# Gate slot first in the first products of the dense stages, zero matmuls behind the sums of six norms, and one pair of loads in the other order

## The reference

```python
def modulated_norm(x, g, shift, scale):
    return rmsnorm(x, g) * (1 + scale) + shift
def swiglu(h, wg, wu, wd):
    return (jax.nn.silu(h @ wg) * (h @ wu)) @ wd
...
    for l in range(DEPTH):                       # DEPTH = 2
        h = modulated_norm(x, norm_g[l, 0], sh1, sc1)
        x = x + 0.5 * g1 * swiglu(h, ffn_wg[l, 0], ffn_wu[l, 0], ffn_wd[l, 0])
        h = modulated_norm(x, norm_g[l, 1], sh2, sc2)
        m = attn_pool_mixer(h, ...) if l % 2 == 0 else short_conv_mixer(h, ...)
        x = x + g2 * m
        h = modulated_norm(x, norm_g[l, 2], sh3, sc3)
        x = x + 0.5 * g3 * swiglu(h, ffn_wg[l, 1], ffn_wu[l, 1], ffn_wd[l, 1])
```

## Time and profile before

| | us |
|---|---|
| median of 3 runs | 1722.42 |
| lowest, highest | 1721.34, 1727.29 |
| the profiled execution, its own time | 1724.32 |
| its span in the profile | 1722.5 |
| PE busy in the span | 1609.0 (93%) |
| mean granted clock of PE | 0.955 |

### The profile page before, as it was taken

How to read it: one execution, slowest core, us unless ns; L and a number is a source line. 1 busy time by engine, 2 the same in 40 slices (tenths; PEclk the granted TensorE clock), 3 DMA queues, 4 the chain that set the end, 5 groups by cost and what they waited for, 6 DMA issues and landing times.

```text
span 1722.5 us, 29138 instructions
## 1 busy us (share of the span) xinstructions
PE 1609.0 (93%) x12267; PEld 1522.4 (88%) x12267; DVE 1130.3 (66%) x1156; ACT 780.7 (45%) x808; POOL 17.2 (1%) x24
## 2 busy tenths in 40 slices
PE   5999989789999999998988999899899889999995
PEld 3999988579999999998988999898788689999994
DVE  2777777567777677756645454664664568888983
ACT  2433344434333443334434333444454447777772
POOL 0000000300000000000000000000000000000000
PEclk8999999889999999999998999999999889999997
DMA  9897766336878587863625555354332518898980
GB/s 323 273 329 278 271 242 242 125 123 248 289 270 313 173 292 270 313 196 126 196 98 171 177 188 177 126 171 117 110 123 98 218 54 347 342 357 346 357 327 26
DMA packets 202482, 379.90 MB, mean 221 GB/s; under 512 B 12185, under 2 KB 157470, under 8 KB 190110
## 3 DMA queue, kind: packets, MB, share of 16 engines
q1 hardware_dynamic: 202398, 378.70, 62.4%
HBM read 377.63 MB, written 1.05 MB: 220 GB/s over the span
## 4 chain that ended last, share of the span: by engine, by line
PE 84%; DVE 7%; ACT 4%; DMA 3%; issue 1%; SPq 0%; ACTq 0%; DVEq 0%
PE ps L579 20%; PE ps L580 19%; PE ps L581 19%; PE ps L1183 3%; PE ps L1185 3%; PE ps L1184 3%; DVE wlo L1678 3%; ACT whi L1300 2%; PE ps L1208 2%; PE ps L1209 2%; PE ps L1210 2%; DMA ada_raw<-in_w_ada_dram 2%; PE ps L690 2%; DVE rstd L1744 1%; PE ps L705 1%
## 5 line engine op out<-in xcount | busy, mean ns | idle before, releaser
L1678 DVE TENSOR_TENSOR wlo<-raw,whi 128x2048 fp32r<-128x2048 f32 (+1 forms) x191 | 432.9, 2267 | 346.5 <-ACT whi L1300 346.4
L579 PE MATMUL ps<-hhi,whi 128*128 128x256 f32 (+1 forms) x2024 | 587.7, 290 | 27.8 <-DVE hlo L1688 16.7
L580 PE MATMUL ps<-hlo,whi 128*128 128x256 f32 (+1 forms) x2024 | 579.1, 286 | 0.0
L581 PE MATMUL ps<-hhi,wlo 128*128 128x256 f32 (+1 forms) x2024 | 578.7, 286 | 0.0
L1300 ACT ACTIVATE whi<-raw 128x2048 fp32r<-128x2048 f32 (+1 forms) x191 | 360.1, 1886 | 209.9 <-PE ps L581 164.2
L579 PEld LDWEIGHTS ps<-hhi,whi 128*128 128x128 f32 (+1 forms) x2024 | 395.1, 195 | 35.8 <-issue 26.5
L580 PEld LDWEIGHTS ps<-hlo,whi 128*128 128x128 f32 (+1 forms) x2024 | 395.1, 195 | 1.8 <-issue 1.4
L581 PEld LDWEIGHTS ps<-hhi,wlo 128*128 128x128 f32 (+1 forms) x2024 | 394.8, 195 | 0.0
L579 PE MATMUL ps<-hidhi,whi 128*128 128x256 f32 x704 | 201.0, 286 | 2.8 <-DVE wlo L1805 2.8
L581 PE MATMUL ps<-hidhi,wlo 128*128 128x256 f32 x704 | 199.2, 283 | 0.0
L580 PE MATMUL ps<-hidlo,whi 128*128 128x256 f32 x704 | 199.2, 283 | 0.0
(11 more groups left out here) (276 smaller groups left out, 2449.7 us busy)
## 6 DMA issues: line engine op xcount, KB each, us to landing
ada_raw<-in_w_ada_dram SPq DMA_DIRECT2D x72, 1024.0 KB, 5.3
raw<-in_ffn_wg_dram SPq DMA_DIRECT2D x44, 1024.0 KB, 5.6
raw<-in_ffn_wu_dram SPq DMA_DIRECT2D x44, 1024.0 KB, 5.4
raw<-in_ffn_wd_dram SPq DMA_DIRECT2D x44, 1024.0 KB, 6.8
raw<-in_w_in_dram SPq DMA_DIRECT2D x18, 1024.0 KB, 5.4
raw<-in_w_exp_gate_dram SPq DMA_DIRECT2D x16, 1024.0 KB, 6.6
raw<-in_w_exp_up_dram SPq DMA_DIRECT2D x16, 1024.0 KB, 8.6
raw<-in_w_exp_down_dram SPq DMA_DIRECT2D x16, 1024.0 KB, 4.8
```

The costliest lines, as they stand in the source:

```text
L579: pe.matmul(o, wh, xh, start=start, stop=False, skip_group_check=shared)
L580: pe.matmul(o, wh, xl, start=False, stop=False, skip_group_check=shared)
L581: return pe.matmul(o, wl, xh, start=False, stop=stop, skip_group_check=shared)
L1678: dve.tensor_tensor(wlo[s][:, 0:width], raw[s][:, 0:width], whi[s][:, 0:width].bitcast(F32), ALU.subtract).then_inc(split[s], 1)
```

## The change

Four edits. (1) In `first_two` the loop over k does both halves of slot 0, with `used[0]` behind it; then comes the wait for slot 1 and both halves of slot 1. The callers wait for slot 1 there and no longer ahead of the loop. (2) `norm_sums` takes a number of matmuls on the tile of zeros (256 columns each, into the free half of bank 6) and runs them behind the sums: 30 ahead of mix0, mix1 and blk2, 18 ahead of ffn1, ffn2 and ffn3, none at the start, ahead of the router and at the end. (3) Before them PE waits for `mod_ready` (the vectors of the modulation that have been turned through bank 6). (4) For ffn3 alone SP issues the first up load (slot 1) ahead of the first gate load (slot 0).

```diff
                 def pair(c):
-                    load(0, c + b[0], wg(c))
-                    load(1, c + b[1], wu(c))
+                    for s in ((1, 0) if stage == "ffn3" and isinstance(c, int) and c == 0 else (0, 1)):
+                        load(s, c + b[s], (wg, wu)[s](c))
...
-            def first_two():
+            def first_two(second):
...
                 for k in range(KT):
                     wait("h_ready")
-                    for s in range(2):
-                        product(s, k, 0)
-                for s in range(2):
+                    for m in range(2):
+                        mm = product(0, k, m, k == 0 and m == 0)
+                mm.then_inc(used[0], 1)
+                second()
+                for m in range(2):
                     for k in range(KT):
-                        mm = product(s, k, 1)
-                    mm.then_inc(used[s], 1)
+                        mm = product(1, k, m, k == 0)
+                mm.then_inc(used[1], 1)

             def first_units(freed_by):
-                for s in range(2):
-                    slot_ready(s)
-                    own(s)
-                first_two()
+                slot_ready(0)
+                own(0)
+                first_two(second=lambda: (slot_ready(1), own(1)))
...
-            def norm_sums():
+            def keep_clock(n, vectors):
+
+                if n:
+                    own(6)
+                    pe.wait_ge(sem("mod_ready"), vectors)
+                for _ in range(n):
+                    pe.matmul(ps[:, 6, T:2 * T], zeros[:, :], zeros[:, :].rearrange("p (o n) -> p o n", o=1).to_broadcast([P, 2, P]),
+                              start=True, stop=True)
+
+            def norm_sums(fill=0, vectors=0):
...
                 mm.then_inc(sem("stat_ready"), 1)
                 frees(7, "stat_read")
+                keep_clock(fill, vectors)
...
-                pe.wait_ge(split[1], b0[1] + 1)
-                if ch:
-                    pe.wait_ge(sem("hid_done"), ch)
-                first_two()
+
+                def second():
+                    pe.wait_ge(split[1], b0[1] + 1)
+                    if ch:
+                        pe.wait_ge(sem("hid_done"), ch)
+
+                first_two(second)
...
-            norm_sums()
+            norm_sums(30, 7)
             first_units(("sq_done", "sq_done"))
...
-            norm_sums()
+            norm_sums(18, 9)
             chunked("ffn1", 9)
-            norm_sums()
+            norm_sums(18, 14)
             chunked("ffn2", 14, 4)
-            norm_sums()
+            norm_sums(30, 18)
...
-            norm_sums()
+            norm_sums(18, 18)
             chunked("ffn3")
-            norm_sums()
+            norm_sums(30, 18)
```

More of the change, by code:

```diff
@@ L601, in feature_major, with product @@
                 mm.then_inc(used[s], 1)
-            def first_two():
-                def product(s, k, m):
+            def first_two(second):
+                def product(s, k, m, start):
                     c = slice(k * 2 * P + m * P, k * 2 * P + (m + 1) * P)
                     return three(ps[:, s, m * T:(m + 1) * T], whi[s][:, c], wlo[s][:, c], hhi[:, k, :], hlo[:, k, :],
-                                 k == 0, k == KT - 1)
+                                 start, k == KT - 1, shared=True)
                 for k in range(KT):
                     wait("h_ready")
-                    for s in range(2):
-                        product(s, k, 0)
-                for s in range(2):
+                    for m in range(2):
[3 more added lines that the diff above has]
+                for m in range(2):
                     for k in range(KT):
-                        mm = product(s, k, 1)
-                    mm.then_inc(used[s], 1)
+                        mm = product(1, k, m, k == 0)
+                mm.then_inc(used[1], 1)
             def first_units(freed_by):
-                for s in range(2):
-                    slot_ready(s)
-                    own(s)
-                first_two()
+                slot_ready(0)
+                own(0)
+                first_two(second=lambda: (slot_ready(1), own(1)))
                 for s in range(2):
```

## The result

| | before | after |
|---|---|---|
| median of 4 runs each, one chip | 1721.88 us | 1704.55 us |
| lowest, highest | 1721.3, 1727.29 | 1700.56, 1705.66 |
| the profiled execution, its span | 1724.32, 1722.5 | 1700.56, 1698.8 |

The ratio of after to before is 0.9892 with a 95% interval of 0.9874 to 0.9911. By the medians the kernel after is 17.3 us faster, where 15.6 were worked out; the interval allows 15.3 to 21.7. The profiled execution is the fastest of the four, 4 us under their median. Of all runs in this document one, of double fill, fell into a slower state of the chip (1784.29 us at a mean clock of 0.833) and is left out of the comparisons. In the kernel after, L1678, L1688, L690, L1323, L1772 and L1300 are L1692, L1702, L700, L1337, L1786 and L1314; L690 is now the fill.

A forecast was written before the change was run, and what follows sets the result against it. PE was taken as the bound, so gains lie where it idles or runs at the lower clock. 7.5 + 6.2 + 1.9 = 15.6 us off the median of 1722.42 gave 1707 us; range 1701 to 1715.

The forecast's parts named there:

- Part 1, what the fill costs: Ahead of six stages' first products: each new zero matmul takes PE 0.12 us, 30 take 3.6, 18 take 2.2, all hidden.
- The rival of a slow fill: Each zero matmul waits for the one before, at 0.38 us; the kernel gets slower, 1737 us; chance 0.03.
- Part 1, what it gives: First products of mix0, ffn1, ffn2, mix1 and blk2: the clock holds, 12.0 us each, 11.6 in blk2; together 7.5 us.
- The rival that the clock falls all the same: In most stages the zeros don't keep the clock up and 7.5 us are lost: 1714.5 us; chance 0.12.
- I take nothing: ffn3's first products: 2.5 us of idle remain behind the zeros, so no clock gain counted; 1.6 us more if it held.
- Part 2, slot 0 first: gate(1) in four dense stages: slot 0 is released earlier, the old wait of 1.75 us goes; 6.2 us gained, ends 5.0 and 7.0.
- the chain of up(1): In ffn2, from silu times up through the hidden parts to the end of slot 1's wlo: 5.47 us.
- The new wait: At up(1), next late once gate(1) no longer waits: 0 to 0.2 us in each of four dense stages.
- Part 3, the swap: Norm ahead of ffn3: with up loaded first, PE's sums run without a stop and end 1.9 us earlier; ends 0 and 1.9.
- more isn't there, since PE ends unit 15 at 897.97: Norm ahead of ffn3: the gain from loading up first can't exceed 1.9 us, as PE's sums can't start sooner.

The follow-up runs named there:

- double fill: The changed kernel with 60 and 36 matmuls on zeros in place of 30 and 18: 1715.04 us over nine runs, ratio 0.9967.
- fill alone: The kernel before plus the matmuls on zeros in six stages and the wait for `mod_ready`, old order of products and loads: 1712.18 us, ratio 0.9954.
- without the swap: The changed kernel with the loads of ffn3 in the old order, gate ahead of up: 1708.95 us, ratio 0.9935.
- after, once more: The changed kernel, nothing altered, measured again on the chip of the kernel with zeros at two more places: 1702.65 us, ratio 0.9894.
- half fill: The changed kernel with 15 and 9 matmuls on zeros in place of 30 and 18: 1708.64 us, ratio 0.9934.
- more fill: The changed kernel with 34 zero matmuls for 18 in ffn3, 40 more in mix0's and 20 in mix1's output products: 1701.53 us, ratio 0.989.
- order alone: The kernel before with only slot 0 first in the first products, no new zeros, old loads: 1714.47 us, ratio 0.997.

## Why the prediction was right, point by point

**The forecast** was 15.6 us less, 1707 in all; measured were 17.3 and 1704.55, inside the range of 1701 to 1715. The mechanism held in both main parts.

**Part 1, what the fill costs.** Right. 0.12 each was taken and 0.12 measured for one more (0.13 on the mean of 18), and PE had 0.2 to 0.5 us left in the five stages that I named. The rival of a slow fill is out. Double fill confirms the price from the other side: 10.5 us for what its sum made 11.4.

**Part 1, what it gives.** Right in five stages: 12.0 us each and 11.6 in blk2 were forecast, 11.97 to 12.00 and 11.64 stand in the windows, and the five gained 7.7 us where 7.5 were written. The rival that the clock falls all the same is out for these: behind at most 0.51 us of idle it held 37 times in 37. One reading under this part was wrong. From the clock of 1.00 in the microsecond from 381, ahead of ffn1, I took that matmuls on zeros count as work. But in that profile the clock stays up through the whole idle piece behind the zeros and goes down only 1.4 us after the first product (383.95). Windows of before:

```profile
383.00:384.00 1.00, 0.05 (x1) 1.00 1.05 422
385.00:386.00 1.00, 1.00 (x8) 0.70 0.07 16
```

So the row shows nothing of the zeros. That they keep the clock is shown by the kernels with and without them.

**ffn3: the step that failed.** "I take nothing" rested on likeness: 2.5 us of idle remain, as much as ffn1 and ffn2 had when they fell. The estimate of the idle piece was right (2.43). The inference that such a piece loses the clock was too sure. Of four profiles with 18 zeros and 2.42 or 2.43 us there, the clock held in three (after, fill alone, without the swap) and fell in one (after, once more). Against the 13.62 us of before the term is 1.66 in the three and 0.48 in the one, about 1.4 on the mean. It is the largest part of what the sum lacked.

**Part 2, slot 0 first.** Right, and the chain step by step: gate(1) had 0.87 us in hand for 0.9 forecast; the chain of up(1) took 602.56 - 597.08 = 5.48 us for 5.47. The new wait is 0.05, in the lower half of the 0 to 0.2 that I gave, so that four stages give 6.8 and not 6.2. By the medians it alone gave 6.0, with an interval that holds both.

**Part 3, the swap.** Right for the profile shown: 1.92 us for 1.9. But "more isn't there, since PE ends unit 15 at 897.97" was bound to that execution. Where mix1 ends earlier, PE comes sooner and the load doesn't, and the swap is worth 3.0 to 3.2. Alone it gave 2.9 by the medians. I had read a distance from one profile as if it were a property of the kernel. The down load, moved up, didn't hold anything up: it landed by 882.46, 8.6 us behind its issue, and ACT stood 5.08 us for it, yet the sums ran without a stop. With gate and down in flight, gate took 5.3 us from issue to landing and down 8.6; with up between them before, gate took 5.4, up 8.0 and down 9.4, and the up load that now goes alone took 5.2. So loads in flight together slow each other, and gate and down landed no later with two than with three. That agrees with the Trainium skill, "DMA: Bandwidth & Descriptors", section "Issuing engines are not separate DMA queues", as cited in the prediction.

**Not foreseen.** In ffn2 some 0.57 us are lost again behind the first products (from up(1) to the next norm's sums 178.8 us for 178.1). They go at the starts of three later gate products (632.66, 668.48 and 704.20), 0.14 to 0.23 at each. Five profiles have 178.8 or 178.9 there and seven 178.1 to 178.3, among these half, double and more fill, which have all edits; the cause stays open. And I took the six norms for the only places with a changing clock, while in these two profiles 6.4 us of the difference come from other places. Against one profile of each kernel 23.7 us would have been read, not 17.3.

## What to carry to other kernels

Idle time of the bound engine that can't be cut can still be filled: matmuls on zeros into a free bank hold the clock for the real work behind. They cost nothing while they fit, and 0.12 us each from the first one that doesn't. Fill until what remains idle is a few tenths of a us: with 2.4 us left, the same steps held the clock in one execution and lost it in another. For a wait that is moved, work out the chain that is late next (here right to 0.05 us), and take a distance between two engines from more than one execution before you call it the kernel's.

## What was not expected of the hardware

The fall of the clock behind one and the same steps isn't fixed. In the twelve profiles, with six norms each, sorted by the idle piece of PE in front of the first product:

| idle ahead of the first product | clock held | clock fell |
|---|---|---|
| 0 to 0.51 us | 37 | 0 |
| 1.29 us | 2 | 0 |
| 2.09 to 2.43 us | 4 | 11 |
| 2.69 to 3.0 us | 1 | 3 |
| 3.5 to 4.6 us | 0 | 14 |

Where the clock fell, the first products took 12.8 to 14.3 us; where it held, 11.5 to 12.0. In two of the 28 falls (ffn3 of before and of order alone) the clock was low already ahead of this idle piece. In ten others it went down 0.6 to 1.5 us after PE had started on the products, as in the windows of 385 and 894 above; a fast first matmul is thus no sign that the clock has held. In the middle rows both results come from one kernel (2.31 us in mix0 and mix1 of the half fill) and from one place in two runs of one program (2.43 and 2.42 us in ffn3). The length of the piece may not be all: between 2.09 and 2.43 us the clock fell 8 times in 8 where no new zeros stood ahead (ffn1 and ffn2), and 3 times in 7 where they did. No run has the same zeros at another place with the idle piece kept, so what the work does and what the shorter idle time does isn't told apart. The Trainium skill, "TensorE: Matmul & The Clock Gate", Part 1, says that the number of matmuls at the slow clock at a kernel's start varies from run to run of the same kernel. These profiles show the like for a clock lost in the middle of a kernel (11.96 and 13.14 us in ffn3 of one program), and that it can also not be lost at all.
